# Gating the feed-forward tiles inside the block-product part instead of in the down projection

## What is computed

```python
def conv_ffn(hn, buf, p):
    t = hn.shape[1]
    u = hn @ p['w_up']
    full = jnp.concatenate([buf.astype(u.dtype), u], axis=1)
    y = p['conv_b']
    for j in range(CONV_W):
        y = y + p['conv_w'][j] * full[:, j:j + t]
    a, g = jnp.split(y, 2, axis=-1)
    return (jax.nn.silu(a) * g) @ p['w_down'], full[:, -(CONV_W - 1):]
```

## Time and profile before

| | us |
|---|---|
| median of 3 runs | 2297.77 (2296.81 to 2298.61) |
| the profiled execution | 2298.68 |
| its span | 2296.9 |
| PE busy | 2231.0 (97%) |
| DVE, ACT, POOL busy | 1522.8, 1145.2, 987.2 |
| DMA queue of SP, share of 16 engines | 32.1% |

### The profile page before, as it was taken

One profiled execution on the slowest core, in us unless ns is written; L12 is line 12 of the kernel. 1 busy time (PEld: TensorE's weight loads), 2 busy tenths in 40 slices (PEclk: granted clock), 3 DMA queues, 4 the chain that ended last, 5 costly groups with the idle time before them and its releaser, 6 DMA issues. The chain is left out here.

```text
span 2296.9 us, 47660 instructions
## 1 busy us (share of the span) xinstructions
PE 2231.0 (97%) x18881; PEld 2109.1 (92%) x18881; DVE 1522.8 (66%) x2518; ACT 1145.2 (50%) x2343; POOL 987.2 (43%) x1165
## 2 busy tenths in 40 slices
PE   7999999999999999999998999999899999969999
PEld 5899999989899999999887999999899999959999
DVE  5667676777777776865887324329866666696663
ACT  6666566657666666664333320125444444454440
POOL 1145352625344444525543224442555555444441
PEclk9999999999999999999999999999999999999999
DMA  7213122221312131211898413111232333353432
GB/s 298 90 54 104 41 79 64 72 82 57 103 54 97 50 101 53 91 45 59 331 352 331 168 45 122 47 47 62 102 107 102 102 106 108 134 192 130 142 106 93
DMA packets 95735, 259.79 MB, mean 113 GB/s; under 512 B 17562, under 2 KB 25626, under 8 KB 95514
## 3 DMA queue, kind: packets, MB, share of 16 engines
q1 hardware_dynamic: 94362, 252.55, 32.1%
q10 hardware_dynamic: 1152, 4.19, 0.4%
HBM read 198.74 MB, written 49.51 MB: 108 GB/s over the span
## 5 line engine op out<-in xcount | busy, mean ns | idle before, releaser
L172 PE MATMUL h_G<-xn_hi,h_w_hi 128*128 128x344 f32 x1368 | 457.3, 334 | 0.2 <-ACT h_d_oraw L918 0.2
L172 PE MATMUL h_G<-xn_hi,h_w_lo 128*128 128x344 f32 x1368 | 437.0, 319 | 0.0
L172 PE MATMUL h_G<-xn_lo,h_w_hi 128*128 128x344 f32 x1368 | 436.6, 319 | 0.0
L1203 POOL TENSOR_TENSOR h_w_lo<-h_w_raw,h_w_hi 128x1024 fp32r<-128x1024 f32 x58 | 149.3, 2575 | 367.6 <-ACT h_w_hi L780 331.9
L172 PEld LDWEIGHTS h_G<-xn_hi,h_w_hi 128*128 128x128 f32 x1368 | 258.3, 189 | 32.6 <-issue 21.2
L172 PEld LDWEIGHTS h_G<-xn_lo,h_w_hi 128*128 128x128 f32 x1368 | 257.1, 188 | 4.6
L172 PEld LDWEIGHTS h_G<-xn_hi,h_w_lo 128*128 128x128 f32 x1368 | 257.0, 188 | 0.0
L3002 DVE SCALAR_TENSOR_TENSOR x<-t_ps,keep_mod,x 128x344 f32<-128x344 f32 x168 | 94.6, 571 | 156.7 <-PE t_ps L2788 93.5
L2788 PE MATMUL t_ps<-f_act_hi,f_d_hi 128*128 128x344 f32 x528 | 170.7, 323 | 19.5 <-POOL f_act_lo L2925 10.7
L2788 PE MATMUL t_ps<-f_act_lo,f_d_hi 128*128 128x344 f32 x528 | 169.9, 322 | 0.0
L2788 PE MATMUL t_ps<-f_act_hi,f_d_lo 128*128 128x344 f32 x528 | 169.4, 321 | 0.0
(11 more groups left out here) (460 smaller groups left out, 7096.0 us busy)
## 6 DMA issues: line engine op xcount, KB each, us to landing
h_w_raw<-in_w_in SPq DMA_DIRECT2D x72, 512.0 KB, 3.7
y_rows<-f_y SPq DMA_DIRECT2D x44, 516.0 KB, 2.8
f_y_in<-y_rows SPq DMA_DIRECT2D x22, 1032.0 KB, 7.0
h_d_ada_w<-in_w_ada SPq DMA_DIRECT2D x32, 512.0 KB, 4.1
g_kp<-in_cache_k SPq DMA_DIRECT2D x32, 512.0 KB, 6.7
g_vp<-in_cache_v SPq DMA_DIRECT2D x32, 512.0 KB, 5.5
f_a<-in_w_ffn SPq DMA_DIRECT2D x57, 256.0 KB, 2.8
h_w_raw<-in_w_mix SPq DMA_DIRECT2D x24, 512.0 KB, 3.6
```

Of the source, the lines that this page charges most:

```text
L172: ins = eng.matmul(out, w[:, k * P:(k + 1) * P], x[:, k, columns], start=(k == 0 and n == 0), stop=(k == n_k - 1 and n == 2))
L1203: pool.tensor_tensor(wlo[w][:, :], raw[r][:, :], whi[w][:, :].bitcast(F32), ALU.subtract).then_inc(lo_done.sem, 1)
```

## The change

1. The gate of a tile f from 2 on is applied in the block-product part. Block p now does for tile p - 1: `silu_raw` on ACT behind the copies of product 5, `cut` on DVE behind the second convolution, `silu` on ACT behind the seeds of bank c, and `gate_act` on DVE behind the low parts of a11 and a22 and before the four additions. It works in place on `y[0]`, with a scratch `e` where part of the rows' low parts lay.
2. `y_store` stores the gated row alone for these tiles (516 KB instead of twice 516), behind `gate_act`; it stands behind the load of a12, not before it. The first tap and the convolution of half 0 of the next tile wait for this store, those of half 1 for `gate_act`.
3. Only tiles 0 and 1 are stored as before and gated in the down projection. The rows are taken in the order 2, 3, ... 21, 0, 1 (`ACTS`, `GROUPS`), so these two come last. Tile 21 is gated in the first down tile, behind its second group of additions (cut behind the first). Of tiles 0 and 1 the cut stands behind the first group of additions of their down tile and the gate behind the second.
4. Rows are read back singly (516 KB) into eight buffers instead of in pairs into four. SP issues six of them in a row behind the store of tile 20 and ahead of the second down weight.
5. The low part of a11 is made before that of a22 (`VECTOR_LOWS`), and in the first block it stands ahead of the low parts of three right operands.

```diff
-VECTOR_LOWS = ("a22", "a11", "a12")
+VECTOR_LOWS = ("a11", "a22", "a12")
...
 def y_store(f):
-    for s in range(2):
-        sp.wait_ge(conved.sem, conved.at(2 * f + s + 1, 0))
-        sp.dma_start(d["y"][2 * f + s], y[s][:, :]).then_inc(y_out[s].sem, 16)
+    if f < GROUP:
+        for s in range(2):
+            sp.wait_ge(conved.sem, conved.at(2 * f + s + 1, 0))
+            sp.dma_start(d[("y", "g")[s]][f], y[s][:, :]).then_inc(y_out[s].sem, 16)
+    else:
+        sp.wait_ge(act_f.sem, act_f.at(gated_at(f), 0))
+        sp.dma_start(d["y"][f], y[0][:, :]).then_inc(y_out[0].sem, 16)
...
 # SP, behind the blocks
-y_load(0)
-y_load(1)
-y_store(LAST - 1)
-down_load(0)
-y_load(2)
-y_load(3)
+act_load(0)
+act_load(1)
+down_load(0)
+y_store(LAST - 1)
+for n in range(2, 8):
+    act_load(n)
 down_load(1)
 down_load(2)
 y_store(LAST)
+gates_load()
...
 # ACT, in block p
     p5_copy(p, s)
+    silu_raw(p - 1)
...
+    silu(p - 1)
...
 # DVE, before block 3
+block_low("a11", STD)
 operand_low(6, 3, 8)
 operand_low(7, 2, 8)
+block_low("a22", STD)
 operand_low(4, 4, 8)
-for n in VECTOR_LOWS:
-    block_low(n, STD)
+block_low("a12", STD)
 for p in range(STD, FT):
     conv(p - 1, 0)
     conv(p - 1, 1)
+    cut(p - 1)
+    if p < LAST:
+        block_low("a11", p + 1)
+        block_low("a22", p + 1)
+    gate_act(p - 1)
     ch.reset()
+    add(p, "c22", 0)
+    add(p, "c22", 1)
+    add(p, "c12", 0)
+    add(p, "c12", 1)
     if p < LAST:
-        block_low("a22", p + 1)
-        block_low("a11", p + 1)
-        add(p, "c22", 0)
-        add(p, "c22", 1)
-        add(p, "c12", 0)
-        add(p, "c12", 1)
         block_low("a12", p + 1)
...
 for t in range(len(DOWN_TILES)):
-    fs = down_acts(t)
+    fs = [LAST] if t == 0 else [ACTS[n] for n in down_acts(t) if ACTS[n] < GROUP]
     for i in range(DOWN_W[DOWN_TILES[t][0]]):
-        f = [v for k, v in enumerate(fs) if k * DOWN_W[DOWN_TILES[t][0]] // len(fs) == i]
-        if f:
-            cut(f[0])
         take(t, i)
-        if f:
-            gate_act(f[0])
+        if i == 0:
+            for f in fs:
+                cut(f)
+        if i == 1:
+            for f in fs:
+                gate_act(f)
```

More of the change, by code:

```diff
@@ L2034 @@
 DOWN_TILES = [(b, w) for b in range(len(DOWN_K)) for w in range(KT // DOWN_W[b])]
+GROUPS = tuple(range(1, N_GROUPS)) + (0,)
+ACTS = [GROUP * g + i for g in GROUPS for i in range(GROUP)]
 DOWN_RING = (0, 1, 6, 7, 2, 3, 4, 5)
@@ L2177, in tail_stage @@
         p5_read = S("p5_read")
-        y_out, y_in = [S(f"y_out{s}", step=16) for s in range(2)], x_in[:4]
+        y_out, act_in = [S("y_out", step=16), S("gate_rows_moved", step=16)], x_in
         d_in, d_hi, d_lo, d_done = [S(f"d_in{i}", step=16) for i in range(3)], S("d_hi"), S("d_lo"), S("down_done")
@@ L2251, in down_bank, with act_at, act_free @@
             return ps[:, DOWN_RING[n % BANKS], 0:TH]
-        def act_at(f):
-            b = max(n for n in range(len(DOWN_K)) if DOWN_F[n] <= f)
-            return b, 0 if b == 0 else 1 + (b + 1) % 2, f - DOWN_F[b]
-        def act_free(eng, f):
-            b, place, row = act_at(f)
+        def act_at(n):
+            b = max(i for i in range(len(DOWN_K)) if DOWN_F[i] <= n)
+            return b, 0 if b == 0 else 1 + (b + 1) % 2, n - DOWN_F[b]
+        def act_free(eng, n):
+            b, place, row = act_at(n)
             if b == 0:
@@ L2357, in down_load @@
                 for i in range(n_g):
-                    src = a["w_ffn"][stored_at("down", DOWN_F[b] // GROUP + i, half), :, q * GROUP * P:q * GROUP * P + out]
+                    src = a["w_ffn"][stored_at("down", GROUPS[DOWN_F[b] // GROUP + i], half), :, q * GROUP * P:q * GROUP * P + out]
                     sp.dma_start(draw[t % 3][:, i * out:(i + 1) * out], src).then_inc(d_in[t % 3].sem, 16)
@@ L2375, in _ @@
             for t in range(len(DOWN_TILES)):
-                for f in down_acts(t - 1) if t else range(2):
-                    if f + 4 < FT:
-                        y_load(f + 4)
+                for n in down_acts(t - 1) if t else range(2):
+                    if n + 8 < FT:
+                        act_load(n + 8)
                 if t + 3 < len(DOWN_TILES):
@@ L2474, in first_tap @@
                     act.wait_ge(block_added.sem, add_at(f, ("c12", "c22")[s], 1))
-                if f:
+                if f > GROUP and s:
+                    act.wait_ge(act_f.sem, act_f.at(gated_at(f - 1), 0))
+                elif f:
                     act.wait_ge(y_out[s].sem, 16 * f)
@@ L2532, in silu, with act_high @@
                 act.activation(e_of(f), e_of(f), ACT.Exp, scale=-1.0).then_inc(e_sig.sem, 1)
-            def act_high(f):
-                b, place, row = act_at(f)
-                act.wait_ge(act_f.sem, act_f.at(f + 1, 0))
-                act_free(act, f)
-                act.activation(ah[place][:, row, :], yin[f % 4][:, 0, :], ACT.Copy).then_inc(act_hi.sem, 1)
+            def act_high(n):
+                b, place, row = act_at(n)
+                act.wait_ge(act_in[n % 8].sem, 16 * (2 + n // 8 + 1))
+                if ACTS[n] < GROUP:
+                    act.wait_ge(act_f.sem, act_f.at(n + 1, 0))
+                act_free(act, n)
+                act.activation(ah[place][:, row, :], yin[n % 8][:, :], ACT.Copy).then_inc(act_hi.sem, 1)
             def down_high(t):
@@ L2646, in _ @@
             first_tap(LAST, 1)
+            silu_raw(LAST)
+            silu(LAST)
             for t in range(len(DOWN_TILES)):
-                for f in down_acts(t):
-                    silu_raw(f)
-                    silu(f)
-                    act_high(f)
+                for n in down_acts(t):
+                    if ACTS[n] < GROUP:
+                        silu_raw(ACTS[n])
+                        silu(ACTS[n])
+                    act_high(n)
                 if t + 2 < len(DOWN_TILES):
@@ L3105, in conv @@
                 st = [old[:, tile, r, :] for r in range(2)]
-                if f:
+                if f > GROUP and s:
+                    dve.wait_ge(act_f.sem, act_f.at(gated_at(f - 1), 0))
+                elif f:
                     dve.wait_ge(y_out[s].sem, 16 * f)
@@ L3253, in program @@
     d = {b: scratch(b, F32) for b in ("oa", "ob")}
[L3254 removed]
+    d["y"], d["g"] = (nc.dram_tensor(n, (k, P, NT), F32, kind="Internal").ap() for n, k in (("act_rows", FT), ("gate_rows", GROUP)))
     d["q_rows"], d["v_rows"] = (nc.dram_tensor(n, (NS, D), F32, kind="Internal").ap() for n in ("q_rows", "v_rows"))
```

113 lines of the change are left out of this document (57 added, 56 removed).

## The result

The changed kernel takes 2314.45 us (median of 4 runs, 2313.22 to 2315.97), the kernel before 2298.19 us beside it (4 runs, 2296.81 to 2301.03). The ratio is 1.0069, with a 95% interval of 1.0052 to 1.0087: slower by 16 us. The forecast was 2307.5 us, +9.7. The profiled execution has a span of 2312.1 us, 15.2 over the 2296.9 before.

What follows compares the result with a forecast made beforehand. TensorE (PE) was taken to bound the kernel, so only its waits count: start +5.9, blocks +17.0, end -13.2, sum +9.7, giving 2307.5 us, range 2292 to 2318.

Steps and rivals of the forecast that it cites:

- The blocks: 17 blocks behind the first: VectorE's addition comes late, PE waits 1.0 us before product 4 in each, +17.0 us.
- The walk: One block's VectorE and POOL instructions timed in turns from its start, ending with product 4 at 18.28 instead of 17.28.
- the first rival: Faster: the gates fit into the blocks, which then cost nothing; 2291 us, or 2280 if the start gains too; chance 0.15.
- The second rival: Half the wait: cut loses its race against POOL's second sum, 0.5 us a block, 8.5 in all, 2299 us; chance 0.15.
- the third rival: Worse: 1.4 us a block and a late second down weight, +21.9 us in all, 2320 us; chance 0.15.
- The start: Up to the start of block 4: earlier first product but later convolution of tile 2, block 4 at 1657.0, +5.9 us.
- The lead: First block: PE starts its first product at 1624.7 instead of 1629.45, 4.7 us sooner.
- the late seeds of product 7: First block: ScalarE issues a seed behind tile 2's exponential, which waits for the convolution; PE waits until 1647.1.
- The end: Last block's start to the last matmul: 286.9 us instead of 300.05, -13.2 us.
- The five places: Waits left in the end: first piece 0.6, piece 6 1.2 (with the piece before), piece 8 3.1, piece 14 3.4, last down group 5.6.
- Piece 6: Down part, pieces counted from 0: waits for a reading ScalarE queued behind the second down weight, 1.2 us with the piece before.
- Piece 14: Down part, pieces counted from 0: waits behind the last tile's gate, 3.4 us, and 1.4 for the clock.

Runs made afterwards that it cites:

- e4: Changed kernel with POOL's low part of s1 made for 8 columns only, product 5 taking that of s3 (low-order terms wrong): median 2297.0 us, ratio to before 0.9987.
- e7: Changed kernel with the cuts of tiles 0 and 1 ahead of the first group of additions and their multiplications behind it: ratio to before 1.0032.
- e3: Changed kernel storing only the first half of each gated row's columns and reading it back twice, second half left out of the result: ratio to before 1.0040.
- e9: Changed kernel with ScalarE's exponential of tile 2 moved behind the two seeds of product 7 in the first block: ratio to before 1.0071.
- e8: Changed kernel with old first-block order, s3's low part at VectorE, gates of tiles 0 and 1 earlier, second down weight loaded ahead of rows 4 to 7: 2281.04 us.

## Why the prediction was right, and where it was off

**The blocks** (+17.0 forecast, +19.2 measured). The walk was right link by link: cut 9.54 (9.6 forecast), POOL's sums 10.70 and 11.94 (10.74, 12.00), low parts 13.7 and 15.4 (13.80, 15.50), multiplications 16.6 and 17.8 (16.64, 17.91), first addition done 18.18 (18.23), product 4 at 18.33 (18.28). That POOL and VectorE take turns, which the first rival doubted, is shown by e4: one POOL instruction out, 17 us gone. The term was short by 0.13 us a block, since I counted it by when product 4 starts and not by what follows a wait: its first half takes 1.51 instead of 1.44, and product 4 starts 1.06 later. (The 0.9 that the profile lists as the wait counts from the end of the matmul before, 0.16 behind the point at which the next one would start.) The prediction named that a wait costs more than its length and then took 1.0.

**The second and third rival.** The second rival said that a block costs 0.5 us less if the cut loses its race against POOL's second sum. In the changed kernel the cut goes first in all 17 blocks, here by 0.11 us (1858.84 and 1858.95), so the forecast's choice was right, on a margin put at 0.05. In one block of e7 the cut loses:

```profile
1837.53 1.79 DVE L3193 TENSOR_SCALAR f_e<-f_e 128x1032 f32<-128x1032 f32 x1
...
1837.29 1.48 POOL L2925 TENSOR_TENSOR f_s<-f_s,f_a 128x512 f32<-128x512 f32 x1 [1.11 <-PE t_ps L2797]
1838.73 1.75 POOL L2927 TENSOR_TENSOR f_s<-f_a,f_s 128x512 f32<-128x512 f32 x1
```

The second sum is shorter, but the third now waits for the cut (1.75 instead of 1.29) and ends 12.14 behind the block's start, where it is 11.97 in the blocks on either side. That block is not shorter than the others (21.37 us, mean 21.30). The cut takes its turn from the one sum or from the other, so the rival's condition could not have saved 0.5 us; what saves 0.43 is a cut that is through before the second sum is due (e3). The later end of the convolution was put at 0.15 us and is 0.11 (8.82 and 8.93 of the block). Of the third rival, neither the 1.4 us a block nor the 8 us for a late weight came.

**The start** (+5.9 forecast, +7.35 measured). The lead (first product at 1624.57, forecast 1624.7) and the late seeds of product 7 were right. The term that was too small is the clock: I allowed 0.4 us once. The granted clock is below full in parts of three stretches of this block, where it is at the lower of its two levels, 1.2 GHz (columns: stretch, length, busy time of PE, PEld, DVE, ACT, POOL, granted clock, DMA share, GB/s):

```profile
1624.50:1630.00 5.50, 5.43 (x32) 5.43 (x33) 5.50 (x3) 2.51 (x4) 5.50 (x3) 0.69 0.11 39
...
1637.00:1648.00 11.00, 5.86 (x37) 5.68 (x37) 10.72 (x12) 3.16 (x6) 6.70 (x5) 0.81 0.08 24
...
1648.00:1656.00 8.00, 8.00 (x50) 8.00 (x50) 5.90 (x9) 4.23 (x7) 2.75 (x3) 0.69 0.19 67
```

The second half of product 1 lasts 2.58 us instead of 1.44, and so do the second halves of products 6 and 7, behind the waits of 2.4 and 5.1 us. Behind the last one 2.7 us are lost. So PE comes to product 4 only at 1655.57, when the addition (forecast for 1653.9) is done: not the addition but the clock sets the end of this block. The wait before product 2 that was forecast until 1638.1 is not there: the low part of a12 is done at 1637.84, about when forecast, but PE comes to product 2 only at 1638.68. The causes stand as told, with one point added by e9: it isn't the seeds that decide but the whole chain behind the late convolution, and moving the seeds alone gains nothing.

**The end** (-13.2 forecast, -11.4 measured). The five places were right: the first piece (0.7 us of wait), pieces 6 (3.0), 8 (2.9) and 14 (1.7), and 5.5 us in the last down block, forecast 5.6. Two sizes were off. Piece 6 was forecast at 1.2 us; it cost 3.0 of wait, and half clock behind the next one, 1.7 us: SP's queue brings the second down weight later than I worked out. It was forecast to land 25.4 us behind the last block's start (2020.29); ScalarE got it 28.3 us behind:

```profile
2048.58 1.06 ACT L2580 ACTIVATE f_d_hi<-f_d_raw 128x1024 fp32r<-128x1024 f32 x1 [9.04 <-DMA f_d_raw<-in_w_ffn]
```

e8, where that load stands ahead of four rows and the wait is gone, agrees. Piece 14, forecast at 3.4 and 1.4 for the clock, cost 1.9 and 0.1. The errors of the end partly cancel: 3.7 us too little for pieces 6 and 8 with their clock, 0.9 too little for the last group, 2.8 too much for piece 14.

So the sign and the mechanism were right, and each of the three terms was too low by 1.4 to 2.2 us. At the start that is what waits cost behind their ends; in the blocks it is half that and half the wait itself; at the end it is the late weight too, less the luck of piece 14.
